# Two-layer encoder on one core: x parked in the output tensor during the FFN blocks, eight load buffers, and another order inside a block

## The reference

```python
def rms_norm(x, g):
    y = x * lax.rsqrt(jnp.mean(x * x, axis=-1, keepdims=True) + EPS)
    return y * g
def swiglu(h, w_gate, w_up, w_down):
    return (jax.nn.silu(h @ w_gate) * (h @ w_up)) @ w_down
for layer in range(2):
    h = rms_norm(x, norm_mix_pre[layer])
    m = mixer(h, ...)                       # even: recurrence and attention; odd: differential attention
    x = x + rms_norm(m, norm_mix_post[layer])
    h = rms_norm(x, norm_ffn_pre[layer])
    f = swiglu(h, w_gate[layer], w_up[layer], w_down[layer])
    x = x + rms_norm(f, norm_ffn_post[layer])
```

## Time and profile before

| what | us |
|---|---|
| median of three runs | 2290.46 (2286.19 to 2292.13) |
| the profiled execution | 2285.69 |
| its span, first to last instruction | 2283.9 |
| PE busy | 2176.9 (95%) |
| DVE busy | 1781.4 (78%) |
| ACT busy | 1470.1 (64%) |
| mean granted TensorE clock | 0.988 |

### The profile page before, as it was taken

One profiled execution on the slowest core, in us unless ns is written; L12 is line 12 of the kernel. 1 busy time (PEld: TensorE's weight loads), 2 busy tenths in 40 slices (PEclk: granted clock), 3 DMA queues, 4 the chain that ended last, 5 costly groups with the idle time before them and its releaser, 6 DMA issues.

```text
span 2283.9 us, 26450 instructions
## 1 busy us (share of the span) xinstructions
PE 2176.9 (95%) x9771; PEld 1768.4 (77%) x9771; DVE 1781.4 (78%) x1554; ACT 1470.1 (64%) x1742; POOL 263.5 (12%) x266
## 2 busy tenths in 40 slices
PE   9999998799999999999999999997999999999996
PEld 7888887677777778877787788785777778777775
DVE  5576566798888999987755656776988998988886
ACT  6677543677767777776656555454767776777663
POOL 0941000600000000000021001016000000000001
PEclk9999999899999999999999999998999999999998
DMA  9555445377676787775564444554676677777663
GB/s 312 169 176 167 165 148 177 121 243 228 209 240 204 219 258 239 235 239 176 184 218 148 148 165 134 183 183 148 201 233 213 210 248 242 234 230 235 207 214 129
DMA packets 219646, 458.48 MB, mean 201 GB/s; under 512 B 12968, under 2 KB 15616, under 8 KB 213888
## 3 DMA queue, kind: packets, MB, share of 16 engines
q1 hardware_dynamic: 213040, 414.29, 52.6%
q0 software_dynamic: 5760, 41.95, 9.4%
q10 hardware_dynamic: 720, 0.56, 0.1%
...
## 4 chain that ended last, share of the span: by engine, by line
PE 58%; DMA 13%; DVE 11%; issue 9%; ACT 5%; POOL 3%; SPq 1%; DVEq 0%; POOLq 0%; ACTq 0%
PE acc L1381 28%; PE acc L1598 11%; DVE w_lo L1669 8%; PE sc L1394 8%; PE pv L1394 4%; DMA raw<-in_ffn_w_down 4%; ACT w_hi L996 3%; DMA raw<-in_ffn_w_gate 3%; PE tp L1408 2%; DMA queries<-in_ffn_w_down 1%; PE acc L1394 1%; DMA gq<-in_ffn_w_gate 1%; PE sc L1494 1%; POOL yacc L2143 1%; DMA queries<-in_ffn_w_up 1%
## 5 line engine op out<-in xcount | busy, mean ns | idle before, releaser
L1669 DVE TENSOR_TENSOR w_lo<-raw,w_hi 128x2048 fp32r<-128x2048 f32 x321 | 737.3, 2307 | 100.7 <-ACT w_hi L996 51.7
L996 ACT ACTIVATE w_hi<-raw 128x2048 fp32r<-128x2048 f32 x321 | 613.1, 1914 | 252.2 <-DMA raw<-in_ffn_w_down 71.6
L1381 PE MATMUL acc<-w_hi,h_hi 128*128 128x512 f32 x936 | 262.4, 402 | 2.1 <-ACT h_hi L966 2.1
L1381 PE MATMUL acc<-w_lo,h_hi 128*128 128x512 f32 x936 | 252.7, 392 | 1.1 <-DVE w_lo L1669 1.1
L1381 PE MATMUL acc<-w_hi,h_lo 128*128 128x512 f32 x936 | 251.3, 390 | 0.1
L1381 PEld LDWEIGHTS acc<-w_lo,h_hi 128*128 128x128 f32 x936 | 175.9, 189 | 39.6 <-DVE w_lo L1669 2.0
L1381 PEld LDWEIGHTS acc<-w_hi,h_lo 128*128 128x128 f32 x936 | 175.6, 188 | 37.8 <-DVE h_lo L1644 0.6
L1381 PEld LDWEIGHTS acc<-w_hi,h_hi 128*128 128x128 f32 x936 | 171.7, 189 | 37.4 <-issue 5.5
L1598 PE MATMUL acc<-w_hi,y_hi 128*128 128x512 f32 x640 | 172.5, 391 | 3.1 <-ACT y_hi L1199 2.9
L1669 DVE TENSOR_TENSOR w_lo<-gx,w_hi 128x2048 fp32r<-128x2048 f32 x70 | 161.0, 2300 | 17.1 <-ACT w_hi L996 13.9
L1669 DVE TENSOR_TENSOR w_lo<-queries,w_hi 128x2048 fp32r<-128x2048 f32 x70 | 161.0, 2300 | 16.9 <-ACT w_hi L996 15.3
(11 more groups left out here) (274 smaller groups left out, 3512.0 us busy)
## 6 DMA issues: line engine op xcount, KB each, us to landing
...
```

The costliest lines, as they stand in the source:

```text
L996: act.activation(w_hi[u % HI][:, :, :], raw[place.buf][:, :, :], ACT.Copy).then_inc(hi_done, 1)
L1381: mm = pe.matmul(acc[n % 2][t][:, :], operand(lhs, a, k, t), w[:, k, :], start=first and k == 0 and j == 0, stop=last and k == KT - 1 and ...
L1669: dve.tensor_tensor(w_lo[u % LO][:, :, :], raw[plan.place[u].buf][:, :, :], w_hi[u % HI][:, :, :].bitcast(F32), ALU.subtract).then_inc(lo_ ...
```

## The change

Its parts:

1. After the last update of x in an FFN's boundary, SP writes `xs` to the output tensor (`spill`, two DMAs of 1 MB), and before the next boundary's first update reads it back (`reload`). Between, the two halves of `xs` are raw buffers 6 and 7. A load into them waits for the spill and for the last readers of x.
2. The early loads are d1, u0, g2 instead of g0, g2, u0; the third, into gq, stands two loads later in SP's queue, at the start of the last two head units.
3. The order of a body's entries, loads, ACT and DVE work is another. Weight sums by DMA are P5A and P7A instead of P7A and P7B; DVE makes P5B, P7B, P6A, P6B, P4A, P4B. Both parts of SiLU and gate stand at the start of the next body.
4. The left sums are DVE's (`left_total`): for pair A four wholes (high + low) and four sums, in the head; for pair B four sums, at the start of body 0. The wholes of chunks 2 and 3 are ACT's: two more copies behind each two of a turn, 16 of 128x128 per layer, into yacc.

```diff
-BLOCK_RAW = 6
+BLOCK_RAW = 8
 POST_GAIN = 5
+SPILLED = 6
...
-ENTRIES = ("P1A", "P1B", "d0", "d1", "P5A", "P5B", "P6A", "P6B", "P3A",
-           "P3B", "P7B", "P7A", "d2", "P2A", "P2B", "d3", "P4A", "P4B")
-DOWNS = ("d0", "d1", "d2", "d3")
-LOADS = ("g0", "g2", "u0", "d0", "u2", "d1", "u1", "u3", "d2", "g1", "d3", "g3")
+ENTRIES = ("P1A", "P1B", "d0", "d1", "P5A", "P5B", "P6A", "P6B", "P3B",
+           "d3", "P7A", "d2", "P7B", "P3A", "P4A", "P2A", "P2B", "P4B")
+DOWNS = ("d0", "d1", "d3", "d2")
+LOADS = ("d1", "u0", "g2", "g0", "d0", "u2", "u3", "d2", "d3", "u1", "g1", "g3")
 EARLY = LOADS[:3]
-FORMS = ("P5A", "P5B", "P6A", "P6B", "P4A", "P4B")
-FORMS_AHEAD = FORMS[:1]
-TRANSFERS = ("P7A", "P7B")
+FORMS = ("P5B", "P7B", "P6A", "P6B", "P4A", "P4B")
+FORMS_AHEAD = FORMS[:0]
+TRANSFERS = ("P5A", "P7A")
 PAIRS = {"A": (0, 1), "B": (2, 3)}
-LEFT = ("S1A", "S3A", "S2A", "S4A", "S1B", "S3B", "S2B", "S4B")
+LEFT = ("S1A", "S2A", "S4A", "S1B", "S2B", "S4B", "S3A", "S3B")
+TOTALS = ("S1A", "S3A", "S2A", "S4A", "S1B", "S3B", "S2B", "S4B")
+HEAD_LEFT = (LEFT[:1], LEFT[1:3])
 LEFT_OF = {"P5": "S1", "P6": "S2", "P7": "S3", "P3": "S4"}
...
-    tasks, before = [], slots[0].u - 1
+    def total(name):
+        return Task("left_total", 2 * body.layer + 1, body.layer, what=name)
+
+    tasks, before = [Task("early_load", src=body, what=EARLY[2])], slots[0].u - 1
     for i, s in enumerate(slots):
         tasks += half(s, 0)
+        tasks += [total(name) for name in (TOTALS[:3] if i == 0 else TOTALS[3:4])]
...
-        tasks += [left(name) for name in LEFT[2 * i:2 * i + 2]]
+        tasks += [left(name) for name in HEAD_LEFT[i]]
...
-    early = [Task("early_load", src=body, what=name) for name in EARLY]
-    return tasks[:ready + 1] + [Task("left_sums", b, layer)] + early + tasks[ready + 1:]
+    early = [Task("early_load", src=body, what=name) for name in EARLY[:2]]
+    return tasks[:ready + 1] + early + tasks[ready + 1:]
...
-    tasks.insert(i + 1, Task("gains", b))
+    tasks[i + 1:i + 1] = [Task("gains", b), Task("reload", b)]
...
-                take((task.src.index, task.what), range(RAW, BLOCK_RAW), released(task.src, task.what))
+                take((task.src.index, task.what), (RAW + EARLY.index(task.what),), released(task.src, task.what))
             elif task.kind == "tile_unit" or task.kind == "half" and task.t == 0 and task.passes[0] == 0:
                 take(task.slot.u, range(RAW), (("lo", task.slot.u + 1, task.slot.u),))
+        for t in range(NT if part.bodies else 0):
+            free[SPILLED + t] = ((("spill", t), part.layer, part.bodies[0].base + 2),)
...
+        raw += [xs[:, t, :].rearrange("p (k n) -> p k n", k=KT) for t in range(NT)]
...
+            def spill(b):
+
+                sp.wait_ge(upd_done, 1 + max(plan.update[b, c, t] for c in range(NC) for t in range(NT)))
+                for t in range(NT):
+                    sp.dma_start(out_rows[:, t, :], xs[:, t, :]).then_inc(spilled[t], 16)
+
+            def reload(b):
+
+                for t in range(NT):
+                    wait_free(plan.after[b // 2 - 1, SPILLED + t])
+                    sp.dma_start(xs[:, t, :], out_rows[:, t, :]).then_inc(x_back[t], 16)
+
...
+                    if k % 2 and task.e in plan.wholes:
+                        for j in (k - 1, k):
+                            kt = KT * task.g + j
+                            ins = act.activation(yacc[:, task.t, kt * P:(kt + 1) * P], input_tile(task.e, j), ACT.Copy,
+                                                 scale=pre[:, task.b, kt:kt + 1])
+                        ins.then_inc(whole_done, 1)
...
                         hi(u)
 
                 if not body.first:
+                    silu_part(body.prev, 0)
+                if not body.first:
                     silu_part(body.prev, 1)
                 high(body, "d1")
-                high(body, "P5A")
                 block_high(body, 0)
                 block_high(body, 1)
+                high(body, "P5A")
+                copy(body, "P1")
                 if body.first:
                     left_high("S1B", body.layer)
                 high(body, "P5B")
-                copy(body, "P1")
                 unload(body, 0, 0)
                 seed(body, 1, 1)
                 unload(body, 0, 1)
+                seed(body, 3, 0)
+                unload(body, 1, 0)
+                seed(body, 3, 1)
+                unload(body, 1, 1)
+                high(body, "P6A")
...
+            def left_total(name, layer):
+
+                pair, done = name[2], len(TOTALS) * layer + TOTALS.index(name)
+                first, second = PAIRS[pair]
+
+                def whole(dst, kg, t):
+                    hi_ap, lo_ap = [m[:, kg * KT:(kg + 1) * KT, t * P:(t + 1) * P] for m in (h_hi, h_lo)]
+                    turn = plan.source["x", 2 * layer + 1, kg, t]
+                    dve.wait_ge(x_hi, turn.m + KT)
+                    wait_event(dve, turn.e)
+                    dve.tensor_tensor(dst.rearrange("p (k c) -> p k c", k=KT), hi_ap.bitcast(F32), lo_ap.bitcast(F32),
+                                      ALU.add).then_inc(left_part, 1)
+
+                s1, s2, s3, s4 = [spare_of[f"S{i}{pair}"] for i in range(1, 5)]
+                if pair == "A":
+                    if name == "S1A":
+                        dve.wait_ge(pv_done, plan.heads_of[layer])
+                        whole(s1, second, 1)
+                        whole(s3, first, 1)
+                        dve.wait_ge(left_part, NC * layer + 2)
+                    elif name == "S3A":
+                        whole(s2, first, 0)
+                        dve.wait_ge(left_part, NC * layer + 3)
+                    elif name == "S4A":
+                        whole(s4, second, 0)
+                        dve.wait_ge(left_part, NC * layer + 4)
+                elif name == "S1B":
+                    dve.wait_ge(whole_done, 8 * (layer + 1))
+                if name[:2] != "S1":
+                    dve.wait_ge(left_sum, done)
+                if name[:2] == "S1":
+                    ins = dve.tensor_tensor(s1, s1, s3, ALU.subtract)
+                elif name[:2] == "S3":
+                    ins = dve.tensor_tensor(s3, s2, s3, ALU.subtract)
+                elif name[:2] == "S2":
+                    ins = dve.tensor_tensor(s2, s1, s2, ALU.add)
+                else:
+                    ins = dve.tensor_tensor(s4, s2, s4, ALU.subtract)
+                ins.then_inc(left_sum, 1)
+
...
+                if task.c == 0 and task.b % 2 == 0:
+                    dve.wait_ge(x_back[task.t], 16 * (task.b // 2))
...
+                form(body, "P5B")
+                if not body.first:
+                    gated(body.prev, 0)
                 if not body.first:
                     gated(body.prev, 1)
                 low(body, "d0")
-                form(body, "P5B")
+                if body.first:
+                    for name in TOTALS[4:]:
+                        left_total(name, body.layer)
                 block_low(body, 0)
                 block_low(body, 1)
                 low(body, "d1")
+                form(body, "P7B")
                 low(body, "P5A")
-                form(body, "P6A")
                 if body.first:
                     left_low("S1B", body.layer)
                 low(body, "P5B")
+                form(body, "P6A")
                 form(body, "P6B")
                 low(body, "P6A")
                 if body.first:
-                    left_low("S3B", body.layer)
                     left_low("S2B", body.layer)
                 low(body, "P6B")
-                low(body, "P3A")
                 if body.first:
                     left_low("S4B", body.layer)
                 low(body, "P3B")
-                low(body, "P7B")
+                low(body, "d3")
+                if body.first:
+                    left_low("S3A", body.layer)
+                    left_low("S3B", body.layer)
                 low(body, "P7A")
                 low(body, "d2")
-                upper_part(body, 0)
                 form(body, "P4A")
+                low(body, "P7B")
+                form(body, "P4B")
+                low(body, "P3A")
+                low(body, "P4A")
                 low(body, "P2A")
                 upper_part(body, 1)
-                form(body, "P4B")
+                upper_part(body, 0)
                 low(body, "P2B")
-                low(body, "d3")
-                low(body, "P4A")
                 low(body, "P4B")
-                gated(body, 0)
                 low_next("P1A")
-                if body.next:
-                    form(body.next, "P5A")
                 low_next("P1B")
...
+                    transfer(body, "P5A")
                     transfer(body, "P7A")
-                    transfer(body, "P7B")
```

More of the change, by code:

```diff
@@ L603, in place_loads @@
         if part.bodies:
-            plan.post_free[part.layer] = [wait[:2] for wait in free[POST_GAIN]]
+            for buf in (POST_GAIN, SPILLED, SPILLED + 1):
```

(7 more changed lines are left out.)

138 lines of the change are left out of this document (67 added, 71 removed).

## The result

The changed kernel takes 2223.6 us (median, 2220.45 to 2225.39) against 2291.3 in the same comparison: ratio 0.9706, 95% interval 0.9687 to 0.9726. The forecast was 2221. Its profiled execution took 2220.45, of which 2218.6 are the span from the first to the last instruction. Of the 65.3 us between the two spans (2283.9 before), 10.7 are PE's busy time (2176.9 before, the same 9771 matmuls, fewer of them slow) and the rest is idle time of PE.

A forecast was written before the change was run, and what follows sets the result against it. TensorE, busy 2176.9 of 2283.9 us, bounds the kernel; only its idle time and slow restarts can be won. 32.5 + 12.0 + 24.4 = 68.9 off 2285.69 makes 2216.8, median 4.8 above: 2221; eight in ten from 2203 to 2252.

The forecast's parts named there:

- Bodies 1 to 8: Bodies 1 to 8 of both layers: every body falls to the 62.2 floor, 32.5 us won (bounds 0 and 45).
- Tails: Last bodies and tails: second turn at 60.1, winning 7.6 and 8.0, less 3.6 for reloads: net 12.0 us.
- the reload: Tail: reading xs back delays the fourth down load by 5.4, costing 1.8 us a layer (bounds 0 and 5.4).
- Boundary, head, body 0: From the boundary to body 1: waits of 9.7 and 8.9 go, smaller ones come; 12.2 us a layer, 24.4 in all.
- the two short waits of 0.5 and 0.7: Boundary: PE waits 0.5 for the high of turn(1,1) and 0.7 for the low of gate chunk 2.
- One sign of being wrong: Head: among the listed signs of a wrong forecast, ACT standing for g0 with PE behind it; no size given.
- the boundary wait: Boundary: 9.7 us once a layer, laid to loads queued on SP behind the third early load, which awaits gq.
- DVE beside POOL: Head: without POOL's sums, DVE lows take 2.28, not 3.38; if the slowdown had another source, 13 us lost, 2235.
- A: Boundaries give nothing: DVE's 12 sums, ACT's 16 copies and the spill replace both waits; 2245, chance 0.13.
- B: Every body: u1 is late, so P6A's and P6B's lows slip 1.3 to 1.9 a body; 2248, chance 0.16.
- D: Slower than before: P5A's DMA sum costs every body a us per us landed past 7.8; 2311, chance 0.05.
- E: Bodies: SP issues in order, so two more buffers bring no loads forward and bodies stay 64.2; 2253, chance 0.07.

The follow-up runs named there:

- e2: Kernel before plus only the two added buffers (eight instead of six) with their store and reload: 2238.8 us, ratio 0.9779.
- e3: Changed kernel restricted to seven buffers, with d2 loaded behind d3 and u1: 2259.9 us, ratio to before 0.987.
- e7: Kernel before with the edits of e1 and e2 together, order and left sums as before: 2213.5 us, ratio 0.9653.
- e1: Kernel before with only its third early load (u0, into gq) two loads later in SP's queue: 2263.2 us, ratio 0.9908.
- e5: Changed kernel with P1A's high on ACT moved behind the last three squares of x in FFN boundaries: 2211.2 us, ratio 0.9642.
- e8: e7 plus squares first, POOL's pair B sums behind the rsqrt, SiLU and tok ahead of P1B's high and low: 2207.5 us, ratio 0.9629.

## Why the prediction was right, point by point

- **The total** is 2.6 us off, in part by luck. Between the profiled executions 68.9 were foretold and 65.3 came: bodies 1.6 less, boundaries, heads and bodies 0 together 2.9 less, 1.7 lost ahead of the first boundary, and tails 2.6 more, which hid part of the rest. (2216.8 + 4.8 is 2221.6, which the forecast gives as 2221.)
- **Bodies 1 to 8: 32.5 foretold, 30.9 measured.** Every body is 62.30, not 62.20, with the one 0.78 wait; the difference is PE's own busy time (61.52 against 61.42). The layout of DVE's work holds: sum P7B was to start at 4.7 after turn 0 and low P6A to end at 19.2; they are at 5.05 and 19.4 (rows 570.37 and 582.44 below, turn 0 at 565.32). But the working did not say which part wins. e2 shows that the buffers alone are enough, and e3 that seven do not do for this order.

```profile
570.37 2.28 DVE L1743 TENSOR_TENSOR raw<-raw,xs 128x2048 f32<-128x2048 f32 x1
582.44 2.29 DVE L1730 TENSOR_TENSOR w_lo<-raw,w_hi 128x2048 fp32r<-128x2048 f32 x1 [0.98 <-ACT w_hi L1045]
```

- **Tails: 12.0 foretold, 14.6 measured (6.5 and 8.1), three sizes off, which cancel in part.** The second turn won 5.7 and 6.1, not 7.6 and 8.0. The tail's first turn now waits 2.7 and stands 61.33 after turn 0 of body 9, the second at 62.0, not 60.1: both SiLUs stand on ACT behind the high of a down load, for which ACT stood 2.74. In e2 and e7 SiLU part 0 comes earlier, and the second turn has 60.19. The fourth down load landed where the working had it, 9.6 after P4B's last matmul at 1060.04 (foretold 9.5), but PE asked for its low only at 1078.95, 5 us after it was made, so the reload cost nothing and not 1.8. Behind the second turn the tails are 0.8 and 2.0 shorter, for which the working had no term: PE is busy 21.12 there instead of 22.04 in layer 0, at a granted clock of 1.00 instead of 0.94, and 22.68 instead of 24.82 in layer 1.

```profile
1055.38 1.07 SPq L892 DMA_DIRECT2D xs<-out  x2
1059.36 1.91 ACT L1045 ACTIVATE w_hi<-raw 128x2048 fp32r<-128x2048 f32 x1 [2.74 <-DMA raw<-in_ffn_w_down]
1069.67 1.92 ACT L1045 ACTIVATE w_hi<-raw 128x2048 fp32r<-128x2048 f32 x1 [4.97 <-DMA raw<-in_ffn_w_down]
1078.95 1.07 PE L1440 MATMUL acc<-w_lo,y_hi 128*128 128x512 f32 x4
```

- **Boundary, head, body 0: 24.4 foretold, 21.5 measured.** Turn 0 was to stand at 432.7; it stands at 435.06, of which 1.7 are from the start. In layer 0 low P1A cost 3.96 (foretold 2.6) and tok 3.00 (3.9), in layer 1 2.75 and 2.32; the two short waits of 0.5 and 0.7 did not come. One sign of being wrong did show, ACT standing for g0 with PE behind it: g0 was to land at 415.0 and landed at 418.33, since up chunk 3's load took 6.5 and not 5.2, and the spills and g0 landed 3.9, 2.2 and 3.1 apart, not 2.7. The cause of the boundary wait is shown by e1, that of what is left by e5. Body 0 is the term that was mis-sized: 67.96 and 66.83 instead of 66.0. The waits in it (0.30, 0.71, 1.20 and 0.78 in layer 0) are 3.0 together, less than the working's 4.3 (2.4, 1.1 and 0.78), though the two at P6A are longer than its 1.1; PE is busy 64.97 and 64.09 for what takes 61.52 at full clock, 3.5 and 2.6 more. Before it was 63.12, 1.7 more. The working had no term for slow matmuls behind the new waits.
- **DVE beside POOL.** With POOL's sums gone, the lows of the head take 2.29 (row 430.85 above; 3.38 before); in e8, with the sums on POOL, a DVE sum of that size takes 3.38 again. The Trainium skill (SBUF — State Buffer, "Who interferes with whom") says that a DVE instruction with two SBUF inputs contends with a GpSimd one that reads SBUF. These traces agree.
- **The rivals.** A is refuted by the table (boundary and head win 12.7 and 13.9). B: DVE never waited for u1 in bodies 1 to 8. D's law is right in kind; its point (6.5, from 7.8) and its price (9.9 a body at 13.8, where the law has 6.0) were too mild. By the Trainium skill (DMA: Bandwidth & Descriptors, "Queues, rings and completion order") each DMA engine alternates packet by packet between the rings that have work, so a sum beside loads should take between 7.0 and 14.0, as an estimate; the 11.8 beside two loads agrees. E is refuted by e2.
